# RWKV-7 chunk scan: the triangular inverse by block row steps on [Z | T], operands grown once per segment, a shorter overflow list and a token-major end

## What is computed

```python
def rwkv_scan(r, decay, k, v, kk, a, s0):
    def step(s, inp):
        rt, wt, kt, vt, kkt, at = inp
        sa = jnp.einsum('bhvk,bhk->bhv', s, -kkt)
        s = s * wt[:, :, None, :] + sa[..., None] * (kkt * at)[:, :, None, :] + vt[..., None] * kt[:, :, None, :]
        return s, jnp.einsum('bhvk,bhk->bhv', s, rt)
...
    for e in range(N_EXPERTS):
        out = out + combine[..., e:e + 1] * swiglu(h, w_gu[e], w_d[e])
...
        x_lat = x_lat + m_lat[5] * rmsnorm(ffn(modulate(x_lat, norm_g[i, 2], m_lat[3], m_lat[4])), norm_g[i, 3])
```

## Time and profile before

| | us |
|---|---|
| median of 3 runs (lowest, highest) | 2986.33 (2985.3, 2987.62) |
| the profiled execution | 2982.42 |
| its span, first to last instruction | 2980.7 |
| PE busy | 2696.9 (90%) |
| DVE busy | 708.3 (24%) |
| ACT busy | 404.5 (14%) |
| mean TensorE clock granted | 0.944 of full |

### The profile page before, as it was taken

The page is one execution under the profiler, slowest core; times in us unless marked ns, Lnnn a source line. Parts: engine busy times, 40 slices in busy tenths (PEclk is TensorE's granted clock), DMA queues, the critical chain, the costliest instruction groups (busy, mean ns, idle before and its releaser), DMA issues.

```text
span 2980.7 us, 67661 instructions
## 1 busy us (share of the span) xinstructions
PE 2696.9 (90%) x30943; PEld 1920.2 (64%) x30944; DVE 708.3 (24%) x1176; ACT 404.5 (14%) x721; POOL 46.9 (2%) x147
## 2 busy tenths in 40 slices
PE   6998887999999679979899869999999999999993
PEld 2553633444444469967799559696968787787861
DVE  1032523000000557745576520000000000000001
ACT  3231102000001322131211120000000000000001
POOL 0000004000000000000000000000000000000000
PEclk9998988999999789989899779999999999999996
DMA  6226018222222300042000239797888888888870
GB/s 230 71 70 254 1 42 288 74 85 71 72 84 71 116 25 4 4 138 69 2 4 4 66 123 345 279 345 280 318 302 319 306 317 306 315 309 317 302 276 15
DMA packets 178923, 493.31 MB, mean 166 GB/s; under 512 B 9362, under 2 KB 73188, under 8 KB 172500
## 3 DMA queue, kind: packets, MB, share of 16 engines
q1 hardware_dynamic: 176852, 482.73, 45.3%
q0 software_dynamic: 1792, 6.19, 0.7%
HBM read 487.84 MB, written 1.05 MB: 164 GB/s over the span
## 4 chain that ended last, share of the span: by engine, by line
PE 85%; DVE 7%; issue 3%; ACT 2%; DMA 1%; SPq 0%; POOL 0%; DVEq 0%; ACTq 0%; POOLq 0%
PE banks L975 23%; PE banks L991 13%; PE banks L585 10%; PE banks L784 10%; PE banks L717 10%; PE banks L727 5%; PE banks L627 2%; PE banks L524 1%; PE banks L948 1%; DVE rstd L1297 1%; PE banks L906 1%; PE banks L960 1%; PE banks L679 1%; PE banks L750 1%; PE banks L761 1%
## 5 line engine op out<-in xcount | busy, mean ns | idle before, releaser
L975 PE MATMUL banks<-ring_arena 128*64 128x112 f32 x14336 | 694.2, 259 | 0.2 <-issue 0.2
L975 PEld LDWEIGHTS banks<-ring_arena 128*64 128x64 f32 x14336 | 687.2, 137 | 9.2 <-issue 8.3
L991 PE MATMUL banks<-ring_arena 128*112 128x512 f32 x896 | 385.8, 592 | 0.0
L784 PE MATMUL banks<-ring_arena 64*64 64x64 f32 x10496 | 328.0, 222 | 44.5 <-DVE ring_arena L1623 17.2
L784 PEld LDWEIGHTS banks<-ring_arena 64*64 64x64 f32 x10496 | 322.3, 138 | 48.8 <-issue 33.3
L585 PE MATMUL banks<-ring_arena 128*128 128x256 f32 (+1 forms) x1024 | 315.0, 471 | 21.7 <-ACT ring_arena L1035 12.7
L717 PE MATMUL banks<-ring_arena 128*128 128x512 f32 x704 | 305.3, 597 | 0.0
L991 PEld LDWEIGHTS banks<-ring_arena 128*112 128x112 f32 x896 | 158.0, 177 | 221.9 <-issue 221.9
L585 PEld LDWEIGHTS banks<-ring_arena 128*128 128x128 f32 x1024 | 199.7, 196 | 137.6 <-issue 96.5
L1787 DVE TENSOR_TENSOR ring_arena<-ring_arena,banks 128x448 f32<-128x448 f32 x32 | 19.9, 621 | 1033.0 <-PE banks L975 1033.0
L717 PEld LDWEIGHTS banks<-ring_arena 128*128 128x128 f32 x704 | 134.8, 192 | 169.8 <-issue 169.8
(11 more groups left out here) (269 smaller groups left out, 1701.9 us busy)
## 6 DMA issues: line engine op xcount, KB each, us to landing
ring_arena<-in_moe_w_gu SPq DMA_DIRECT2D x256, 896.0 KB, 5.5
ring_arena<-in_moe_w_d SPq DMA_DIRECT2D x112, 1024.0 KB, 7.1
ring_arena<-in_mod_w SPq DMA_DIRECT2D x48, 1024.0 KB, 7.2
ring_arena<-in_ff_w_gu SPq DMA_DIRECT2D x22, 1024.0 KB, 5.2
ring_arena<-in_rw_w_rkv SPq DMA_DIRECT2D x20, 1024.0 KB, 11.0
ring_arena<-in_gla_w_in SPq DMA_DIRECT2D x12, 1024.0 KB, 5.6
ring_arena<-in_ff_w_d SPq DMA_DIRECT2D x11, 1024.0 KB, 4.9
ring_arena<-in_gla_w_out SPq DMA_DIRECT2D x4, 1024.0 KB, 13.6
```

What stands on the lines that cost most here:

```text
L784: ins = T.matmul(ps[4 * d + b][r, p * CH:p * CH + CH], lhs[r, p, :], EYE2[r, :] if rhs is None else rhs[r, p, :], start=first and p == 0, ...
L975: ins = T.matmul(bank[CH * h:CH * h + CH, (c % 4) * CAP:(c % 4) * CAP + CAP], w[:, kk, c * P + CH * h:c * P + CH * h + CH], XG[:, 2 * kp + ...
L991: ins = T.matmul(ps[6 + h][0:CAP, :], HX[:, 2 * u + k, :], w[:, k, 512 * h:512 * h + 512], start=(u == 0 and k == 0), stop=(u == WD_UNITS ...
```

## The change

The inverse is now formed on Z0 = [Z | I] (128 columns for each pair, two banks for each direction): the raw product of AA and [A | I] gives the removal product and its transpose-side copy in one call, and level l multiplies the masked, transposed block row matrix SL into [Z | T]. Between two levels VectorE masks Z out of the bank (`level_mask`) and transposes the mask (`level_turn`), while ScalarE copies the 128 columns to ZT (`level_out`). Level 5 works on 64 columns with S5, made by two block transposes. PK = KD·[A | I] gives Lak and Kt together. `heads` has a new argument `cross`: the pairs 4 to 7 write to the other half of the partitions, so that they lie on the off-diagonal quadrants. The chunk sums, the exponentials and the products by them are made once per segment; U1 and its products stand ahead of the latent scan. The overflow list has MORE_ITEMS = (2·256 − 1)/112 = 4 places, the last scatters stand ahead of its loop, and the end is computed token by token: the residual stream is transposed during the router, the squares are summed by ScalarE along the row, the post gain is laid out as a row by a product with a diagonal, and four DMAs store the result. The diff, cut to its core:

```diff
-MORE_ITEMS = (PARTS - 1) * NE
+MORE_PARTS = (PARTS - 1) * NE
+MORE_ITEMS = (2 * SEG - 1) // CAP
...
-                n = eng.value_load(more_i[0:1, bass.ds(x + MORE_ITEMS, 1)], min_val=NE, max_val=NE + MORE_ITEMS)
                 with eng.If(over > 0):
-                    item(x, n)
+                    item(eng.value_load(more_i[0:1, bass.ds(x + MORE_ITEMS, 1)], min_val=0, max_val=MORE_PARTS - 1), x + NE)
             return eng.value_load(more_i[0:1, 2 * MORE_ITEMS:2 * MORE_ITEMS + 1], min_val=NE, max_val=NE + MORE_ITEMS)
...
+        def scan_banks(d, half):
+            return two_banks(4 * d + 2 * half)
...
-            def heads(d, b, lhs, rhs, first=True, last=True):
+            def heads(d, half, lhs, rhs, cross, first=True, last=True):
...
                 for p in range(HP):
-                    for r in rows:
-                        ins = T.matmul(ps[4 * d + b][r, p * CH:p * CH + CH], lhs[r, p, :],
-                                       EYE2[r, :] if rhs is None else rhs[r, p, :],
-                                       start=first and p == 0, stop=last, skip_group_check=True)
+                    for r in range(2):
+                        x = rhs[rows[r], p, :]
+                        ins = T.matmul(bank[rows[1 - r if cross and p >= HP // 2 else r], p, 0:x.shape[-1]],
+                                       lhs[rows[r], p, :], x, start=first and p % (HP // 2) == 0, stop=last,
+                                       skip_group_check=True)
                 return ins
...
+            def raw(d, g):
+                pe.wait_ge(fr_s[d], FRS.value(g // SC, g % SC, "A"))
+                heads(d, 0, pick(AA[d], d, g), WORK[d][f"AI{g % 2}"], True).then_inc(raw_pe[d], 1)
+
+            def level(d, lat, i, l):
+                w = WORK[d]
+                if l == 0:
+                    pe.wait_ge(zv_s[d], ZVS.value(lat, i, "t0"))
+                    pe.wait_ge(bt_act[d], SC * lat + i + 1)
+                    heads(d, 0, w["SL"], w["Z0"], True).then_inc(lv_s[d], 1)
+                elif l < 5:
+                    pe.wait_ge(zv_s[d], ZVS.value(lat, i, f"t{l}"))
...
+                    for d in range(2):
+                        pe.wait_ge(dv_s[d], DVS.value(lat, i, "Lak"))
+                        if i < 2:
+                            pe.wait_ge(S["vt_out"], 4 + 2 * i + d + 1)
+                        pe.wait_ge(fr_s[d], FRS.value(lat, i, "R"))
+                        heads(d, 1, pick(AA[d], d, g), w[d]["R"], True).then_inc(pe_s[d], 1)
+                levels(2)
+                pe.wait_ge(S["vt_out"], 4 * lat + 2 * min(i, 1) + 2)
+                for d in range(2):
+                    pe.wait_ge(dv_s[d], DVS.value(lat, i, "Mrb" if lat else "Lak"))
+                    heads(d, 1, w[d]["Lak"], V[d], False, last=False).then_inc(pe_s[d], 1)
+                levels(3)
+                for d in range(2):
+                    pe.wait_ge(pe_s[d], PES.value(lat, i, "LakV"))
+                    heads(d, 1, AI[d][:, :, 0:CH], w[d]["ST"], True, first=False).then_inc(pe_s[d], 1)
+                levels(4)
...
+                    for d in range(2):
+                        pe.wait_ge(ac_s[d], ACS.value(lat, i, "W"))
+                        heads(d, 1, KX[d], w[d]["R"], True).then_inc(pe_s[d], 1)
+                levels(5)
                 if i < SC - 1:
...
+                    for d in range(2):
+                        raw(d, g + 1)
+                for d in range(2):
+                    pe.wait_ge(za_s[d], ZAS.value(lat, i, "C5"))
+                    heads(d, 1, w[d]["TT6"], w[d]["W"], False).then_inc(pe_s[d], 1)
...
+                        pe.wait_ge(ac_s[d], ACS.value(lat, i, "SA"))
+                        heads(d, 1, w[d]["ST"], w[d]["R"], False, last=False).then_inc(pe_s[d], 1)
+                    for d in range(2):
+                        pe.wait_ge(pe_s[d], PES.value(lat, i, "y0"))
+                        heads(d, 1, V[d], w[d]["Mrk"], True, first=False, last=False)
+                        heads(d, 1, w[d]["SA"], w[d]["Mrb"], True, first=False).then_inc(pe_s[d], 1)
+                for d in range(2):
                     if lat:
-                        step(d, 1, [(w[d]["ST"], R[d]), (V[d], w[d]["Mrk"]), (w[d]["SA"], w[d]["Mrb"])], [])
+                        pe.wait_ge(dv_s[d], DVS.value(lat, i, "y"))
+                    else:
+                        pe.wait_ge(ac_s[d], ACS.value(lat, i, "SA"))
+                    heads(d, 1, w[d]["Kt"], V[d], True, last=False)
+                    heads(d, 1, w[d][f"Bt{g % 2}"], w[d]["SA"], True, first=False).then_inc(pe_s[d], 1)
 
             for sg in range(2):
                 segment(sg)
                 if sg == 0:
                     pe.wait_ge(S["st_zero"], 2)
-                removal_product(SC * sg)
+                pe.wait_ge(S["keys_b"], 4 * (sg + 1))
+                pe.wait_ge(S["ident_a"], 2 * (sg + 1))
+                for d in range(2):
+                    raw(d, SC * sg)
+                pe.wait_ge(S["ident_z"], 6 * (sg + 1))
                 for i in range(SC):
...
+            pe.wait_ge(S["post_done"], 3 * KT)
+            for q in range(4):
+                if q >= 2:
+                    pe.wait_ge(S["h_tm_out"], q - 1)
+                for k in range(4 * (q % 2), 4 * (q % 2) + 4):
+                    ins = T.transpose(ps[(6 + q) % 8][:, (k % 4) * P:(k % 4) * P + P],
+                                      X[:, k, SEG + q // 2 * P:SEG + q // 2 * P + P], ident[:, :])
+                ins.then_inc(S["res_t"], 1)
+            pe.wait_ge(S["gain_diag"], 1)
+            for h in range(2):
+                pe.wait_ge(S["h_tm_out"], h + 3)
+                T.matmul(ps[2 + h][:, :], ones[:, :], GAIN_DIAG[:, 4 * h:4 * h + 4, :],
+                         start=True, stop=True).then_inc(S["gain_mm"], 1)
...
                 if q < 2:
-                    pe.wait_ge(S["yd_out"], 2 * n)
+                    pe.wait_ge(S["yd_out"], 2 * n + 2)
...
-                    ins = T.matmul(ps[4 + q % 2][:, (k % 2) * SEG:(k % 2) * SEG + SEG], YS[0:CAP, k * P:k * P + P],
-                                   PWT[0:CAP, :], start=True, stop=True)
-                ins.then_inc(S["sc"], 1)
-
-            def item(n):
+                t, h = q // 2, q % 2
+                T.matmul(ps[4 + h][:, :], PWT[0:CAP, t * P:t * P + P], YS[0:CAP, 512 * h:512 * h + 512],
+                         start=True, stop=True).then_inc(S["sc"], 1)
+
...
-                    ins.then_inc(S["out_t"], 1)
+                scatter(NE, q)
+
+            def more(x, n):
...
+                for d in range(2):
+                    act.wait_ge(S["sums"], 2 * SC * sg + SC * (d + 1))
+                    C.activation(flat4(E3[d]), flat4(SG[d]), ACT.Exp, scale=DECAY).then_inc(S["e3"], 1)
+                for d in range(2):
+                    act.wait_ge(S["e3"], 2 * sg + d + 1)
+                    C.activation(flat4(SG[d]), flat4(SG[d]), ACT.Exp, scale=-DECAY).then_inc(S["e2"], 1)
...
+                def level_out(l):
+                    for d in range(2):
+                        act.wait_ge(zv_s[d], ZVS.value(lat, i, f"S{l + 1}" if l < 4 else "S5b"))
+                        half = slice(0 if l < 4 else CH, 2 * CH)
+                        C.copy(w[d]["ZT"][:, :, half], scan_banks(d, 0)[:, :, half]).then_inc(za_s[d], 1)
+                level_out(0)
+                for d in range(2):
+                    act.wait_ge(pe_s[d], PES.value(lat, i, "PK"))
...
+                    if j == 2:
+                        sums(sg)
                     if j == 3:
+                        if sg == 0:
+                            rates(0)
+                            grown((KD[0], AA[0], KD_TMP, AA[1]), 0)
                         keys(sg)
-                directions(sg)
...
+            def grown(tensors, sg):
+
+                for n, v in enumerate(tensors):
+                    dve.wait_ge(S["e3"], 2 * sg + n // 2 + 1)
+                    ins = Vv.tensor_tensor(flat4(v), flat4(v), flat4(E3[n // 2]), ALU.mult)
...
+            def level_mask(d, lat, i, l, src):
+                w = WORK[d]
+                Vv.tensor_tensor(w["S"], src, over(LM[l][d]), ALU.mult).then_inc(zv_s[d], 1)
+
+            def level_turn(d, lat, i, l):
+                w = WORK[d]
+                dve.wait_ge(zv_s[d], ZVS.value(lat, i, f"S{l}"))
+                Vv.transpose(flat2(w["SL"]), flat2(w["S"])).then_inc(zv_s[d], 1)
+
+            def start(g):
+                lat, i = g // SC, g % SC
+                for d in range(2):
+                    w = WORK[d]
+                    dve.wait_ge(raw_pe[d], g + 1)
+                    Vv.tensor_tensor(w["Z0"][:, :, 0:CH], scan_banks(d, 0)[:, :, 0:CH], over(STRICT[d]), ALU.mult).then_inc(zv_s[d], 1)
+                    dve.wait_ge(zv_s[d], ZVS.value(lat, i, "Z0a"))
+                    Vv.tensor_tensor(w["Z0"][:, :, 0:CH], w["Z0"][:, :, 0:CH], EYES, ALU.add).then_inc(zv_s[d], 1)
+                    dve.wait_ge(zv_s[d], ZVS.value(lat, i, "Z0b"))
```

(43 more changed lines are left out.)

539 lines of the change are left out of this document (255 added, 284 removed).

## The result

The changed kernel takes 2833.47 us (median of 4 runs, 2828.18 to 2834.78) against 2985.82 us, a ratio of 0.9487 (95% interval 0.9471 to 0.9504): 152 us or 5.1% less, where the forecast was 2861 with a range that ended at 2843. Its profiled execution has a span of 2830.9 us, 149.8 under the 2980.7 of before.

What follows compares the result with a forecast made beforehand. Scans were taken as bound by TensorE with short waits for VectorE, the tail as a chain of latencies. 2982.4 - 77.7 - 4.5 + 3.5 - 46.5 = 2857.2 us, plus 3.9 for the median: 2861, range 2843 to 2912.

Steps and rivals of the forecast that it cites:

- The look-ahead: Scans: TensorE looks ahead over about four records, so a crossed call takes 12 steps, not 16; chance 0.62, 2861 us.
- the author's walk: Scans: three engine queues carried forward in program order with durations from profile rows; trusted to some 3%.
- The middle between 20 and 29.2 ns of issue: Scans: unknown whether four records can start in one 58.4 ns step; took 310.5 us, ends 303.7 and 319.3.
- The surcharge: Scans: time above the walk; of the remaining 10 us, 5 kept (bounds 0 and 10).
- Strict order, the first rival,: Scans: matmuls start in program order, 14 steps for a crossed call, wide 1.53 us; 2879 us, chance 0.17.
- No quadrant overlap: Scans: rival in which crossed calls keep 16 steps, scans 359.7 us; 2910 us, chance 0.15.
- Crossed quadrants that disturb each other: Scans: rival in which cross quadrants disturb each other in the banks, each step alone; 3054 us, chance 0.04.
- The rest of the change in the scans: Scans: the gain without any quadrant overlap, 33.5 us (393.2 less 359.7).
- Moved ahead of the scan: Segments before the scans: sums, rate operations, products and exponentials moved there cost nothing, covered by idle VectorE time.
- Behind the scan: After the latent scan: U1's sum and products no longer hold the first bonus matmul; 4.5 us gained (3.0 to 5.5).
- The router: After the logits: added transposes and copies delay the exponential and position matmuls; 3.5 us lost (1 to 6).
- The end: Tail after the experts: scatters ahead of the overflow loop, 18 us instead of 64.5; 46.5 us gained (43 to 49).

Runs made afterwards that it cites:

- runs of one: Changed kernel with the pairs in the order 0, 4, 1, 5, 2, 6, 3, 7, so diagonal and off-diagonal products alternate: 2825.0 us.
- runs of two: Changed kernel with the pairs in the order 0, 1, 4, 5, 2, 3, 6, 7, two diagonal then two off-diagonal: 2820.3 us.
- run 32: Not a run label: "run" is a verb here, four quadrants process 32 matmul records in 0.87 us (128 columns) or 0.47 us (64).

## Why the prediction was wrong, step by step

**The look-ahead: right mechanism, wrong size, and this is the miss.** The prediction read from the earlier trace rows that a stream on new quadrants starts while two matmuls (four records) of the old one are ahead of it, and took four as the depth for all shapes: 12 steps for a crossed call. The runs show the time of 7 records gained at each change for wide calls (9.2 steps) and of 6 for narrow ones (10 steps). The row was of another shape, tiles of 64 rows by 128 columns with 256 moving, of which one works at a time; in the scans two work side by side. There the change gains 3.5 records of one tile, here 3.4 or 3.0 steps of a pair: counted in steps the row was nearly right for the scans, and halving it, by counting its records over both tiles, is where the miss comes from. By the author's walk a depth of six gives 278.6 us instead of 302.6: 24 of the 27 us. The bounds of the unknown covered the issue of records but not the depth itself; with eight records as its other end (266.8 us by the same walk), the range would have begun some 36 us lower, and held the result.

**The middle between 20 and 29.2 ns of issue.** 29.2 ns is what a pair on two tiles leaves in the earlier trace rows, no floor: the two records of a pair start 6 or 7 ns apart in the changed kernel and already in the trace of the kernel before, and runs of one pass at 14.6 ns. Taking the middle cost 6.8 us (310.5 against 303.7; the middle of 303.7 and 319.3 is in fact 311.5, a slip of 1 us in the sum).

**The surcharge.** 5 us were kept for clock and lead-ins. The changed kernel stands 7.7 us above the walk with six records. The stops in the middle of calls are 1.9 us of it. The larger part is a clock that falls after a wait within a chunk, which the prediction had named as a sign of being wrong. Behind the 2.18 us in which TensorE waits for SA in the second context chunk, the four products of the state run at the 1.2 GHz level (length, busy, clock):

```profile
1176.30:1177.30 1.00, 1.00 (x40) 0.50 0.07 16
1177.30:1178.30 1.00, 1.00 (x41) 0.50 0.00 0
```

and take nearly 1 us each instead of 0.58. It falls behind five of the waits for SA in the two scans. In the latent scan three calls behind that wait take 3.64 us with such a fall and 2.18 us in the first chunk, where none came: 1.5 us each time, and by this estimate some 7 us for the five. Without the crossing the wait of the second context chunk is 1.05 us long and the clock stays (same columns):

```profile
1186.74:1190.50 3.75, 3.75 (x128) 1.00 0.02 4
```

So a part of what the quadrants win is given back here, which the walk didn't have. The length of the wait alone doesn't decide it: with runs of two a wait of 2.34 us up to 1206.86 us was followed by 4 us at clock 1.00.

**Strict order, the first rival,** is refuted: it forbids wide calls under 1.53 us. The rule of the Trainium skill that stood beside it (TensorE: Matmul & The Clock Gate, What happens when you issue a matmul: only weight loads are pulled ahead, matmuls start in strict order) doesn't hold between quadrants, as the six overtaken records show. **No quadrant overlap** would have been 359.7 us for the scans, and the run without crossing gives 360.2 on TensorE, so the walk itself was sound. **Crossed quadrants that disturb each other** are refuted by the same runs of one, in which all four are busy at once: 8 steps.

**The rest of the change in the scans** was 30.4 us against 33.5 forecast. The chunk periods: context 31.0 us (forecast 33.1), latent, behind the first two chunks, 36.9 to 37.5 (38.5). L0 came 6.0 us after the context lead-in began (5.9) and 8.5 us in the latent one (8.8).

**Moved ahead of the scan, at nothing:** right, the latent segment is no longer than before, and VectorE's cover held.

**Behind the scan** 6.0 us (4.5, at most 5.5): right in its mechanism, a little more in size. **The router** 3.5 us (3.5): right too; the exponential was the term, 7.1 us behind the logits, and moving it forward returned 2.1 us.

**The end** was 3.6 us short, just outside its bounds (42.9 for 43 to 49). The turns were rightly read as the "issue" of the earlier trace rows. What failed is the sentence that put TensorE's scatters ahead of the loop and then left the loop: its queue still has to run, behind the last scatter nothing hides it, and its jumps cost 3.8 and 7.1 us where the forecast had seen only turns of 2.06 us. It cost 5.4 us.

With the measured scans (288.4 for 315.5), the stretch behind them (1.5 us less) and end (21.6 for 18) the same sum gives 2861 - 27.1 - 1.5 + 3.6 = 2836 us, for a median of 2833.5.

## What to carry to other kernels

Small fp32 tiles on different quadrants of the array run side by side as far as the engine sees ahead, six records on two tiles here: order the products so that neighbours lie on different quadrants, in runs of one or two matmul pairs, rather than block by block; it costs a line. When a resource of the chip is known from one row of another shape, ask in what unit it was counted there, here records of one tile, and let the range carry that number's own uncertainty, not only that of the terms around it. A wait that the profile calls "issue" can still be a semaphore's: look at what the engine's queue does in that time. A loop that is never taken belongs to the sum of every engine whose queue ends with it: ask what the last instruction of each queue is, and put one condition around the whole.

## What the runs showed of the hardware that wasn't expected

- TensorE starts fp32 matmuls of 64x64 tiles out of program order across quadrants: a new pair of tiles starts while six records of the old pair have still to start, and with one tile of 64x128 at work it is three. Each change gains the time of 7 records with 128 columns moving, of 6 with 64. Four quadrants at work run 32 records in 0.87 us (128 columns) or 0.47 us (64).
- A straight-line program can outrun its instructions: gaps of 0.3 to 1.8 us between starts, at multiples of 127 matmul records, each ending 1.2 to 1.5 us after a packet of instructions has landed (with runs of two). They cost 1.9 us in the changed kernel's scans and 10.0 to 17.4 us in the faster orders, and 12 of 19 stay at the same record when 32 records are put ahead.
- A skipped body of a loop costs TensorE 3.8 us by its first jump and 7.1 us with the output's transfer under way, and the output's DMAs land in 3.4 us instead of 2.1 beside it.
- Behind five waits for SA of 2.1 to 2.2 us the granted clock fell to the 1.2 GHz level for most of the following microseconds (mean 0.57 over 4.0 us in the context); behind those of 1.05 us it did not, nor behind one of 2.34 us in another order.
